# Long convolution of 31 taps: three taps move to GpSimd, seventeen stay on VectorE, eleven plus an identity product on TensorE

## The reference, cut to what matters

```
def even_mixer(h, w_in, sc_conv_w, cf_conv_w, cf_conv_b, cf_ln_g, cf_ln_b, w_out):
    z = h @ w_in
    sc_b, sc_c, sc_x, cf_a, cf_g = jnp.split(z, [...], axis=-1)      # 512 channels each
    y_sc = sc_b * causal_dwconv(sc_c * sc_x, sc_conv_w)              # 3 taps
    u = cf_a * jax.nn.sigmoid(cf_g)
    u = causal_dwconv(u, cf_conv_w) + cf_conv_b                      # 31 taps
    u = jax.nn.silu(layernorm(u, cf_ln_g, cf_ln_b))
    return jnp.concatenate([y_sc, u], axis=-1) @ w_out
```

## Time and profile before

| | |
|---|---|
| median of 3 runs | 1589.12 us (1587.17 to 1589.21) |
| the profiled execution | 1587.2 us, of which the span of instructions is 1585.3 us |
| TensorE busy | 1548.7 us, 98% |
| VectorE busy | 1258.3 us, 79% |
| ScalarE busy | 850.5 us, 54% |
| GpSimd busy | 52.4 us, 3% |
| mean granted TensorE clock | 0.997 of full speed |

### The profile page before, as it was taken

The page is one execution under the profiler, slowest core; times in us unless marked ns, Lnnn a source line. Parts: engine busy times, 40 slices in busy tenths (PEclk is TensorE's granted clock), DMA queues, the critical chain, the costliest instruction groups (busy, mean ns, idle before and its releaser), DMA issues. The chain is left out here.

```text
span 1585.3 us, 26715 instructions
## 1 busy us (share of the span) xinstructions
PE 1548.7 (98%) x10882; PEld 1436.4 (91%) x10884; DVE 1258.3 (79%) x1592; ACT 850.5 (54%) x1014; POOL 52.4 (3%) x61
## 2 busy tenths in 40 slices
PE   9999999999999999999999999999999998999998
PEld 7989999998898999999999899999999998899997
DVE  7988898777489897888888697888888888685555
ACT  6665554664465455644455564445544456564443
POOL 1010000100010000000000010000000000100000
PEclk9999999999999999999999999999999999999999
DMA  8514986454148875588844258885688844255551
GB/s 300 208 33 179 344 295 243 153 202 134 54 160 312 312 253 189 201 326 304 308 174 164 92 201 324 319 307 196 235 313 308 316 163 145 96 193 183 188 190 70
DMA packets 59805, 344.24 MB, mean 217 GB/s; under 512 B 6800, under 2 KB 7312, under 8 KB 28752
## 3 DMA queue, kind: packets, MB, share of 16 engines
q1 hardware_dynamic: 58752, 340.93, 60.5%
q0 software_dynamic: 544, 1.97, 0.3%
q10 hardware_dynamic: 432, 0.27, 0.1%
HBM read 342.09 MB, written 1.05 MB: 216 GB/s over the span
## 5 line engine op out<-in xcount | busy, mean ns | idle before, releaser
L1457 DVE TENSOR_TENSOR wl<-raw,wh 128x2048 fp32r<-128x2048 f32 (+2 forms) x256 | 569.8, 2229 | 136.8 <-ACT wh L1027 134.8
L678 PE MATMUL PS<-HP,wh 128*128 128x512 f32 x1728 | 608.1, 396 | 2.1 <-DVE wl L1457 2.1
L1027 ACT ACTIVATE wh<-raw 128x2048 fp32r<-128x2048 f32 (+2 forms) x256 | 475.5, 1860 | 143.8 <-PE PS L763 120.7
L679 PE MATMUL PS<-HP,wl 128*128 128x256 f32 x1728 | 484.7, 281 | 0.0
L678 PEld LDWEIGHTS PS<-HP,wh 128*128 128x128 f32 x1728 | 324.3, 188 | 76.9 <-DVE wl L1457 2.5
L763 PE MATMUL PS<-FX,wh 128*128 128x256 f32 x1920 | 344.5, 282 | 0.0
L679 PEld LDWEIGHTS PS<-HP,wl 128*128 128x128 f32 x1728 | 326.6, 189 | 0.0
L763 PEld LDWEIGHTS PS<-FX,wh 128*128 128x128 f32 x1920 | 294.9, 189 | 2.3
L763 PE MATMUL PS<-FX,wl 128*128 128x256 f32 x960 | 270.1, 281 | 0.0
L763 PEld LDWEIGHTS PS<-FX,wl 128*128 128x128 f32 x960 | 180.8, 188 | 0.0
L1556 DVE SCALAR_TENSOR_TENSOR ada<-ada,AR 128x1024 f32<-128x1024 f32 x144 | 172.9, 1219 | 0.0
(11 more groups left out here) (270 smaller groups left out, 1678.8 us busy)
## 6 DMA issues: line engine op xcount, KB each, us to landing
raw<-weights SPq DMA_DIRECT2D x242, 1024.0 KB, 5.0
ada<-ada_w SPq DMA_DIRECT2D x144, 512.0 KB, 6.0
raw<-weights SPq DMA_DIRECT2D x6, 768.0 KB, 4.3
raw<-weights SPq DMA_DIRECT2D x4, 576.0 KB, 5.0
X<-x SPq DMA_DIRECT2D x2, 512.0 KB, 5.6
raw<-weights SPq DMA_DIRECT2D x2, 512.0 KB, 6.8
out<-Z SPq DMA_DIRECT2D x4, 256.0 KB, 2.4
CN<-shape_constants SPq DMA_DIRECT2D x1, 587.0 KB, 12.6
```

Of the source, the lines that this page charges most:

```text
L678: mm(pairs(bank(bk)), lhsT=lhs(0, k), rhs=HP[:, k], start=k == 0, stop=False, skip_group_check=True)
L679: last = mm(bank(bk, 0, S), lhsT=lhs(1, k), rhs=HH[:, k, :], start=False, stop=k == k_tiles - 1, skip_group_check=True)
L1027: last = A_(dst(wh), src, ACT.Copy)
L1457: last = tt(dst(wl), src, dst(wh).bitcast(F32), ALU.subtract)
```

## The change

VectorE keeps taps 0 to 16, TensorE makes taps 17 to 27, and GpSimd makes taps 28 to 30. For each tile GpSimd multiplies the three slices by their weight columns, which are broadcast along the free axis, and adds them up in `T[:, 4 + t]`: three products and two sums of 128 x 256 for each tile, twenty instructions in all. It starts when `U` is complete and the first norm's values in `T` are no longer needed. TensorE adds each finished tile to its PSUM sum by a product with the identity, the last of the tile's group. `conv_sum` waits for these instead of for the taps. VectorE's short products (L1812) stay four taps ahead of its last one.

```
-DVE_TAPS = 19
+DVE_TAPS = 17
+POOL_TAPS = 3
...
-        pe_taps = [(t, k) for t in range(4) for k in range(DVE_TAPS, TAPS)]
+        pe_taps = [(t, k) for t in range(4) for k in range(DVE_TAPS, TAPS - POOL_TAPS)]
...
             pool.dma_start(AR[:], A["c_2"].unsqueeze(0).to_broadcast([P, D])).then_inc(c_in, 16)
+            pool.wait_ge(z_out, 3)
+            pool.wait_ge(ev("cf_in"), 2)
+            pool.wait_ge(hh_ready, 4)
+            pool.wait_ge(h_ready, 4)
+            U = cols(Z, EV["U"], 4, 30 + S)
+            for t in range(4):
+                for k in range(TAPS - POOL_TAPS, TAPS):
+                    w, first = pc("cfw", 4 * k + t).to_broadcast([P, S]), k == TAPS - POOL_TAPS
+                    dst = T[:, 4 + t, :] if first else WK[:, 3072 + S * ((2 * t + k - TAPS) % 4):][:, 0:S]
+                    pool.tensor_tensor(dst, U[:, t, k:k + S], w, ALU.mult).then_inc(ev("cf_step"), 1)
+                    if not first:
+                        steps = t * (2 * POOL_TAPS - 1) + 2 * (k - TAPS + POOL_TAPS)
+                        pool.wait_ge(ev("cf_step"), steps)
+                        ins = pool.tensor_tensor(T[:, 4 + t, :], T[:, 4 + t, :], dst, ALU.add)
+                        ins.then_inc(ev("cf_step"), 1)
             for name in ("ffn0", "mix1"):
                 add_squares(name)
...
-                   start=k == DVE_TAPS, stop=k == TAPS - 1).then_inc(ev("cf_tap"), 1)
+                   start=k == DVE_TAPS, stop=False).then_inc(ev("cf_tap"), 1)
+                if k == TAPS - POOL_TAPS - 1:
+                    pe.wait_ge(ev("cf_step"), (t + 1) * (2 * POOL_TAPS - 1))
+                    mm(bank(4 + t // 2, (t % 2) * S, S), lhsT=cn("ident"), rhs=T[:, 4 + t, :],
+                       start=False, stop=True).then_inc(ev("cf_full"), 1)
...
-                dve.wait_ge(ev("cf_tap"), (i + 1) * len(pe_taps) // 2)
+                dve.wait_ge(ev("cf_full"), 2 * i + 2)
```

## The result

The changed kernel takes 1595.76 us (median of 7 runs, 1593.53 to 1596.90) against 1589.12 us (7 runs, 1587.17 to 1589.97). The ratio is 1.0039, 95% interval 1.0027 to 1.0051: it is slower by 6.6 us. The profiled execution of the changed kernel was the longest of its seven, 1596.9 us with a span of 1595.1 us, against 1587.2 and 1585.3.

The account below looks back on a forecast made before the run. VectorE's chain was taken to set the convolution stage's end, with TensorE nearly full behind it: +9.8 - 3.2 = +6.6 us, so 1589.12 + 6.6 = 1595.7 us. Range 1590.5 to 1601.5; the forecast by itself 1594 to 1599.

Parts of the forecast that it names:

- VectorE's chain sets the stage's end: Long convolution: VectorE reaches conv_sum(1) after TensorE's taps end at 90.09, so TensorE's last sums start only at 92.90.
- -3.2 us for eight taps: VectorE's chain in the convolution: two taps of four tiles fewer, 8 x 0.396 = 3.2 us off.
- TensorE, ScalarE and the waits on GpSimd cost nothing: Convolution: 48 TensorE products become 44 + 4, ScalarE's saving is hidden, GpSimd ends near 65, before 74.0 when first needed.
- 20 x 0.49 = 9.8 us: Convolution: each of twenty GpSimd instructions holds VectorE for 0.49 us, the price measured for sums beside L1476.
- the lower bound: Broadcast products as short as a memset allows hold VectorE 0.07 us each; all twenty GpSimd instructions then cost 4.7 us.
- 6.6 us at conv_sum(0): VectorE's net delay at conv_sum(0), +9.8 - 3.2 = +6.6 us: start at 96.8 instead of 90.24.
- TensorE waits 0.5, 4.0 and 0.6 us for low parts, beside VectorE's chain: TensorE before its taps, units n0+7 to n0+9: 5.1 us of waits for `lo`, in slack, not added.
- The clock: TensorE idling, as 2.4 us before conv_sum(0), may halve its clock: 1.7 us, left out of the forecast, kept in the range.
- That GpSimd doesn't hold VectorE up: Rival, convolution from 42.85 to about 63: the 3.2 us stand, gain capped at 1.9 us, 1587.2 us; chance 0.07.
- The reading by which each costs its whole length: Rival, convolution: each GpSimd instruction costs VectorE 0.73 us or more, +14.6 - 3.2 = +11.4, 1600.5 us; chance 0.16.
- That a product costs less than a sum: Rival, convolution: GpSimd's broadcast products are short, +4.7 - 3.2 = +1.5 us, 1590.6 us; chance 0.11.
- GpSimd was never late: Rival, convolution: GpSimd becomes the bound above 2.6 us per instruction, TensorE waits for identity products, 1600 us; chance 0.04.

Follow-up runs that it names:

- with the zeros: Changed kernel plus eight bf16 products of zeros in an unused bank behind TensorE's last identity product: 1593.99 us, ratio 1.0023.
- GpSimd beside the kernel before: Kernel before plus GpSimd's twelve products and eight sums into four unused buffers, nothing waiting for them: 1600.06 us, ratio 1.0063.

## Why the prediction was right, and where it was off

The forecast was 1595.7 us and the median is 1595.76. The mechanism was the forecast one: GpSimd's reads of SBUF hold up VectorE's chain, which sets the end of the stage. The agreement to 0.1 us is luck: one term was 1.5 us too large, and one that is there in some executions, at 2.3 us in the profiled one, was left out.

- *VectorE's chain sets the stage's end.* Right. Without GpSimd's reads the stage gained 2.1 us, where 1.9 was worked out, with conv_sum(1) capped by TensorE's last product. The medians differ by 3.1 us, and that more is not explained.
- *-3.2 us for eight taps.* Right; the spacing is 0.396 us wherever GpSimd is idle.
- *TensorE, ScalarE and the waits on GpSimd cost nothing.* Right; no wait on GpSimd, whose work ended at 62.3 (near 65 predicted).
- *20 x 0.49 = 9.8 us.* Right in kind, too large in size: 8.3 us. The rows had sums only. Products cost 0.36 us, sums 0.52 us, and 12 x 0.36 + 8 x 0.52 = 8.5 us. The working named the product as unmeasured and took the sum's price "since they are the same instruction with the same number of inputs"; that was the step that failed. The measured price of a product lay between that value and the lower bound.
- *6.6 us at conv_sum(0).* 5.15 us of the stage, and 0.5 us that this execution was behind ahead of it: 95.89 instead of 96.8.
- *TensorE waits 0.5, 4.0 and 0.6 us for low parts, beside VectorE's chain.* 0.3 and 3.1 us, and none ahead of the third. The taps still ended at 94.4, ahead of conv_sum(0), so they added nothing, as forecast.
- *The clock.* Left out of the sum and kept in the range at 1.7 us. It fell in the profiled execution behind the 2.2 us wait and cost 2.3 us there. The prediction looked at two waits, of 3.2 and 4.6 us, and at the window at 882, where it read 1.00. It missed the fall at 862 in the same trace, behind a wait of 2.56 us, which was the nearest row for the 2.4 us wait that it worked out. The range by itself (1594 to 1599) held four of the seven runs; three were just under it, at 1593.5 to 1593.7.
- *The rivals.* That GpSimd doesn't hold VectorE up fell with the taps at 0.80 us. The reading by which each costs its whole length, 0.73 us, fell with the 0.42 us measured: a period of 0.80 us is shorter than a tap's 0.396 us and GpSimd's 0.61 to 0.74 us one after the other, so they overlap in part; in which part is not shown. That a product costs less than a sum was right, 0.36 against 0.52 us, and the 0.07 us of the lower bound was not. GpSimd was never late.

A sum behind it that the prediction did not make: three taps of a tile cost VectorE 3 x 0.396 = 1.19 us if it makes them, and on GpSimd they are three products and two sums that hold it for 3 x 0.36 + 2 x 0.52 = 2.1 us. As long as VectorE's instructions read two tensors from SBUF, giving it this work back is cheaper than being relieved of it.

## What to carry to other kernels

Ahead of moving elementwise work from VectorE to GpSimd, look at how many inputs VectorE's instructions in that stretch read from SBUF, and find a row where the two already ran side by side: the price is in the rows of VectorE, not of GpSimd. Where the running sum could live in a free PSUM bank, the taps and GpSimd no longer collided, and VectorE lost less than 1 us to it. A piece of work taken off one chain must be put where its engine really has room; the end of the first feed-forward layer looked idle and was not. And a single trace's end can be off by a clock that fell at another place: compare the shift of one instruction behind the stage.

## What the runs showed of the hardware

- VectorE's taps with one input and the output in PSUM keep the spacing of those in SBUF: eight in 3.22 us against 3.25 us. With one input in PSUM and the output in SBUF four take 1.64 us beside GpSimd's reads.
- GpSimd's memset of 128 x 256 beside VectorE's taps with two tensor inputs costs them nothing (1.66 us for four, as before), and beside tap 0, a tensor_scalar with one, it costs a little (1.65 us for four against 1.38). Its reads cost 0.36 to 0.52 us each, and tap 0 was held up by them too (2.59 us).
- The clock fell behind waits of TensorE of 2.2 us and 4.65 us (changed kernel) and of 2.56 us (kernel before), and within waits of 3.1 us (with the zeros) and 4.1 us (GpSimd beside the kernel before). It did not fall at the 3.1 us wait of the changed kernel nor at the 3.2 us one of the kernel before. The length of a wait alone does not tell.
